# Moving the query and key rotation one chunk later in the recurrence of a hybrid decoder layer

## The chip, the cores and the metric

The kernel runs on one core of a Trainium2 chip, as one launch. The metric is the device time of that launch in microseconds (us). Before the change it was run three times: 2240.45, 2242.23 and 2244.01 us, median 2242.23 us. A further execution, recorded by the hardware profiler, took 2243.18 us by the same clock.

## The reference, cut to what matters

One layer, 1024 prompt tokens and 8 sample tokens together (1032 columns), model width 1024, float32. Each layer normalises its input with a condition-dependent scale and shift, multiplies by a wide input matrix, and runs two mixers on the result: attention with 8 heads, and a gated linear recurrence with 8 heads. Only the parts that the change touches:

```
qa = rope(rmsnorm(qa) * q_norm_g, pos); ka = rope(rmsnorm(ka) * k_norm_g, pos)   # per head, 2 halves of 64
oa = rmsnorm(attend(qa, ka, va)) * subln_g * 0.8                                  # per head, 128 wide
# recurrence over chunks of tokens, per head (S is the 128x128 state):
cum = cumsum(g); A = (q * decay) @ k;  o = A @ v + (q * exp(cum)) @ S
S   = exp(cum[-1]) * S + (k * exp(cum[-1] - cum)).T @ v
```

The rotation (rope) needs, for a piece of q or k: a multiplication by cos, a copy of the piece with its 32-row quarters exchanged, a multiplication of that copy by sin, a sum, and last a multiplication by the reciprocal root of the mean square, which comes from a product with a block matrix.

## The kernel before, in words

Every large product is done in three float32r products of split operands (high x high, high x low, low x high): one *piece* is 8 blocks of 3 products with 344 output columns, 24 products on TensorE (`product`, L172).

The first stage (`norm_stage`) normalises the input. TensorE adds up the squares (L350), makes the condition's scale and shift by `ada(k)` (L364, 32 small products) and `pick(k)` (L372), and in a loop over k = 0..7 issues `ada(k+3)`, `pick(k+2)` and `pieces(k)` (L385, 18 products, which need the k-th block of the normalised input, high and low: L337 on ScalarE, L474 on VectorE).

The second stage (`heads_stage`) goes over the 8 heads h. Each head has an attention part and then a recurrence part of 8 chunks k = 0..7 of 128 tokens. The dense pieces for later use are spread between them; in the recurrence chunk k carries one piece, `REC_PIECES[k]`. For heads 0 to 6 these are the queries, keys and values of the next head: piece u = 0..5 (three of q, three of k) is computed in the chunk before k = 0 (u = 0) and in chunk k = u - 1, the three of v in chunks 5, 6, 7. Head 7 has no next head (`no_next`).

Each engine has its own program in order, and waits on semaphores by hand; no planner is involved. In chunk k:

- **TensorE** waits for the operands of the chunk (`lv_k`, then L1192), makes the small products L1192 to L1202, transposes (L1207), before the change then adds up the squares of piece k - 1 (`qk_sums`, L1058 and L1059), computes its dense piece (L172), and closes with L1228 to L1232 (output and new state).
- **ScalarE** computes the decay levels of the next chunk (L916 to L922), copies the transpose (`kht`, L1015), finishes the levels (L927, L928), makes the high part of a square (L933), turns the sums into a reciprocal root (`qk_norm`, L818 and L820), then reads the dense piece out of PSUM (for q and k: square L813 and copy into `rg[u % 3]` L814), and copies the chunk's output (L1037).
- **VectorE** runs `assemble` (L1485 to L1492, after `kht`), `operands` of the next chunk (L1476, L1477), then before the change `squares_low` (L1508), `rope` (L1361, L1363) of piece k, `rope_end` (L1367) of piece k - 1, and `state` (L1500 or L1503).
- **GpSimd** computes level differences two chunks ahead (L1278, L1279) and multiplies the piece by cos (L1319). **SyncE's queue** issues the DMAs: the exchanged copy of a piece (`turn`, L706, four DMAs) once the piece is read and a `squares_low` is done, and the load of condition weights (L725).

Piece u is read into `rg[u % 3]`, one of three buffers. ScalarE may overwrite it when `rope_end` of piece u - 3 is done. That wait stands in the part of `piece` that reads q and k:

```
u = n - 12
act.wait_ge(qk_ready.sem, qk_ready.at(h, max(u - 2, 0)))
if u >= 2:
    act.wait_ge(sq_low.sem, sq_low.at(h, u - 1))
qk_piece(gq if kind == "q" else gk, bank, sq[u % 2][:, :], rg[u % 3][:, :])
```

`qk_ready` counts the `rope_end`s; these lines are not part of the diff. In the last chunk TensorE also adds up the squares of the attention's output (`attention_sums`, L1125 and L1126), inside the dense piece, and ScalarE makes the reciprocal root (L944, L946). Then the next head's `scores_of` (L1113) and `turn8` (L1119) follow.

Of the kernel before, what the change touches and what calls it, by code (L numbers as in the profile page):

```python
# [40 lines left out]
H = 8  # L41
# [155 lines left out]
def norm_stage(nc, a, c, x, hi, lo, mem, early, banks):  # L197
# [7 lines left out]
    with Stage(c) as ctx:  # L205
# [139 lines left out]
        @block.tensor  # L345
        def _(pe):
            def sums(p):
                pe.wait_ge(paired.sem, p + 1)
                for j in range(NP):
                    ins = pe.matmul(SP_[:, j, 0:TH], mean[:, :], sq[2 * p % 4][:, cols(j)], start=(p == 0), stop=(p == KT // 2 - 1))  # L350
                    if p == KT // 2 - 1:
                        ins.then_inc(summed.sem, 1)
                if p < KT // 2 - 1:
                    ins.then_inc(ms_used.sem, 1)

            def ada(k):

                if k >= 2:
                    pe.wait_ge(mod_in.sem, k - 1)
                for n in (2 * k, 2 * k + 1):  # L360
                    pe.wait_ge(ada_in[n % RING].sem, 16 * (n // RING + 1))
                    for r in range(KT):
                        quarter = slice(r % 4 * QUAD, (r % 4 + 1) * QUAD)
                        ins = pe.matmul(X[quarter, k % 2, n % 2 * P:(n % 2 + 1) * P], c["csil"][:, r, :],  # L364
                                        aw[n % RING][:, r * P:(r + 1) * P], start=(r < 4), stop=(r >= 4))
                ins.then_inc(ada_done.sem, 1)

            def pick(k):
                pe.wait_ge(ada_read.sem, k + 1)
                for n in range(2):  # L370
                    at = PICK_COL + n * QUAD
                    ins = pe.matmul(X[:, k % 2, at:at + CS], av[k % 2][:, n * P:(n + 1) * P], c["pick"][:, 0:CS], start=True, stop=True)  # L372
                ins.then_inc(picked.sem, 1)

            def pieces(k):

                pe.wait_ge(high.sem, k + 1)
                pe.wait_ge(low.sem, k + 1)
                w = slice(k * P, (k + 1) * P)
                for n, (t, j) in enumerate(EARLY_PIECES):  # L380
                    if k == 0 and j == 0:
                        pe.wait_ge(w_hi.sem, t + 1)
                        pe.wait_ge(w_lo.sem, t + 1)
                    for q, (wp, xp) in enumerate(((early["hi"], hi), (early["hi"], lo), (early["lo"], hi))):
                        pe.matmul(first[n], wp[t][:, w], xp[:, k, cols(j)], start=(k == 0 and q == 0), stop=(k == KT - 1 and q == 2))  # L385

            pe.wait_ge(mean_in.sem, 16)
            for p in range(KT // 2):
                sums(p)
            pe.wait_ge(csil.sem, 1)  # L390
            ada(0)
            ada(1)
            pe.wait_ge(pick_ready.sem, 1)
            pick(0)
            ada(2)
            pick(1)
            pe.wait_ge(lnd.sem, NP)
            for k in range(KT):
                if k + 3 < KT:
                    ada(k + 3)  # L400
                if k + 2 < KT:
                    pick(k + 2)
                pieces(k)

        @block.gpsimd
# [106 lines left out]
HIGH_AT = (4, 5)  # L512
SQUARES_AT = 6
SUMS_AT, SUMS_BEHIND = 7, 3
KEYS_AT = (3, 4, 5, 7)


# [21 lines left out]
def heads_stage(nc, a, o, c, d, xh, xl, early, banks, gate):  # L539
    with Stage(c) as ctx:  # L540
# [57 lines left out]

        def sum_bank(h, u):

            return u % 2 if u < 2 or h == H - 1 else 1

        def half(u):

            return slice((u % 2) * 512, (u % 2) * 512 + 512)

        def square_high(h, u):

            return osq_hi[1 if u >= 2 and h < H - 1 else 0][:, half(u)]
# [57 lines left out]
        def no_next(h):  # L667

            return h == H - 1
# [132 lines left out]
        def _(act):  # L802
# [137 lines left out]
            def o_norm(h, u):  # L940

                act.wait_ge(o_summed.sem, o_summed.at(h, u + 1))
                r = rstd_o[:, (u % 2) * 512:(u % 2) * 512 + 512]
                ch(act.activation(r, X[:, sum_bank(h, u), :], ACT.Ln, bias=c["eps"][:, 0:1]))  # L944
                ch.sync()
                act.activation(r, r, ACT.Exp, scale=-0.5).then_inc(o_rstd.sem, 1)  # L946

# [104 lines left out]
        def _(pe):  # L1052
# [54 lines left out]
            def scores_of(h, i):  # L1107
                nk = (i + 1) * P
                for m in range(2):
                    rows = slice(DH * m, DH * (m + 1))  # L1110
                    for b in range(0, nk, 512):
                        w = min(512, nk - b)
                        ins = pe.matmul(SP_[:, score_bank(i, m) + b // 512, 0:w], qT[rows, i * P:(i + 1) * P], kT[rows, b:b + w],  # L1113
                                        start=True, stop=True)
                ins.then_inc(scores.sem, 1)
# [6 lines left out]
            def o_sum(h, u):  # L1122
                pe.wait_ge(o_squared.sem, o_squared.at(h, u + 1))
                pe.wait_ge(o_high.sem, o_high.at(h, u + 1))
                pe.matmul(X[:, sum_bank(h, u), :], ones[:, :], square_high(h, u), start=True, stop=False)  # L1125
                pe.matmul(X[:, sum_bank(h, u), :], ones[:, :], osq_lo[:, half(u)], start=False, stop=True).then_inc(o_summed.sem, 1)  # L1126

            def attention_sums(h):
                if no_next(h):
                    pe.wait_ge(rows_ready.sem, 1)  # L1130
                else:
                    pe.wait_ge(qk_ready.sem, qk_ready.at(h, 6))
                o_sum(h, 0)
                o_sum(h, 1)

            for h in range(H):
                pe.wait_ge(qk_ready.sem, qk_ready.at(h, 0))
                scores_of(h, 0)
                pe.wait_ge(piece_read.sem, piece_read.at(h, 0))
                if h:  # L1140
                    pe.wait_ge(o_rstd.sem, o_rstd.at(h - 1, 2))
                turn8(Xf, vT).then_inc(v_turned.sem, 1)
                pe.wait_ge(o_read.sem, o_read.at(h, 0))
                pe.wait_ge(st_ready.sem, st_ready.at(h, 0))
# [38 lines left out]
                for k in range(NB):  # L1183
# [21 lines left out]
                    if REC_PIECES[k][0] in ADA_AT:  # L1205
                        ada(h, REC_PIECES[k][0])
                    pe.transpose(kht_ps, K[:, 0, :], ident[:, :]).then_inc(rec_done.sem, 1)  # L1207
                    if 0 < k <= 6 and not no_next(h):
                        pe.wait_ge(sq_high.sem, sq_high.at(h, k))
                        pe.wait_ge(sq_low.sem, sq_low.at(h, k))  # L1210
                        if k >= 3:
                            pe.wait_ge(qk_ready.sem, qk_ready.at(h, k - 2))
                        qk_sums((k - 1) % 2)
                    for n in REC_PIECES[k]:
                        piece(h, n, (SUMS_BEHIND, attention_sums, h) if k == SUMS_AT else None)
                    if k == 1 and no_next(h):
                        pe.wait_ge(sample_qkv.sem, sample_qkv.at(h, 1))
                        pe.wait_ge(sample_rec.sem, sample_rec.at(h, 1))
# [23 lines left out]
        def _(pool):  # L1242
# [53 lines left out]
            for h in range(H):  # L1296
# [16 lines left out]
                for k in range(NB):  # L1313
# [13 lines left out]
                    if k == SQUARES_AT:  # L1327
                        pool.wait_ge(pv_read.sem, pv_read.at(h, NB))
                        pool.wait_ge(o_normed.sem, o_normed.at(h, 0))
                        if not no_next(h):  # L1330
                            pool.wait_ge(qk_ready.sem, qk_ready.at(h, 5))
                        squares(h, oraw, 0)
                        squares(h, oraw, 1)
                    for n in REC_PIECES[k]:
# [13 lines left out]
        def _(dve):  # L1348
# [172 lines left out]
            for h in range(H):  # L1521
# [31 lines left out]
                for k in range(NB):  # L1553
                    assemble(h, k)
                    if k + 1 < NB:
                        operands(h, k + 1)
                    if k == 0:
                        use_sigmoid(h, len(SIGMOID) - 1)
                    if k == 7:
                        o_norm(h, 0)  # L1560
                        o_norm(h, 1)
                    if k < 6 and not no_next(h):
                        u, j = k, k % NP
                        if k:
                            squares_low(h, k)
                        dve.wait_ge(qk_cos.sem, qk_cos.at(h, u + 1))
                        dve.wait_ge(qk_turned[u].sem, qk_turned[u].at(h, 4))
                        rope(j, rg[u % 3][:, :], rt[u % 2][:, :])
                    if 0 < k <= 6 and not no_next(h):
                        u = k - 1  # L1570
                        dve.wait_ge(qk_rstd.sem, qk_rstd.at(h, u + 1))
                        if u == 0:
                            dve.wait_ge(sample_qkv.sem, sample_qkv.at(h, 1))
                            dve.wait_ge(kv_stored.sem, kv_stored.at(h, 2))
                        rope_end(u % NP, X[:, u % 2, 0:TH], rg[u % 3][:, :], qT if u < 3 else kT)
                    state(h, k)
                ch.reset()

# [2047 lines left out]
```

## Time and profile before

| | us |
|---|---|
| three runs, median (lowest, highest) | 2242.23 (2240.45, 2244.01) |
| the profiled execution, its own time | 2243.18 |
| its span, first to last instruction | 2241.4 |
| TensorE busy, products | 2210.7 (99%) |
| TensorE weight loads | 2100.9 (94%) |
| VectorE busy | 1557.2 (69%) |
| ScalarE busy | 1175.5 (52%) |
| GpSimd busy | 939.0 (42%) |
| the head read below, recurrence chunks 0 to 7 | 402.80 to 452.19 |

Busy time of TensorE is made of modelled ends, and small products overlap, so a short wait hides in it. For waits one reads the distance between the starts of instructions. The busy shares of the other engines are means over stages with different limits. The head read below is h = 2; times of rows are microseconds from the start of the span.

### The profile page before, as it was taken

To read this page: it belongs to the slowest core of one execution; us is meant where nothing else is said; L and a number is where in the kernel's file an instruction comes from. 1 tells how busy PE (TensorE), PEld (TensorE's weight loads), DVE (VectorE), ACT (ScalarE), POOL (GpSimd) and SP (SyncE) were. 2 spreads that over 40 slices of the span, in tenths; PEclk is the share of its full clock that TensorE was granted. 3 is DMA by queue.
4 is the path that set the end of the run, shared out by engine and by line. 5 is a ranking of instruction groups with operands and counts; after the bars stand their busy time and mean duration, and the time that the engine had idled before them with its cause. 6 is when DMAs were issued, how large, how long until landed. Compare 5 with 4: busy or idle time off the path is not lost. (4 is left out here: it accounts for less than half of the span.)

```text
span 2241.4 us, 47969 instructions
## 1 busy us (share of the span) xinstructions
PE 2210.7 (99%) x18881; PEld 2100.9 (94%) x18881; DVE 1557.2 (69%) x2574; ACT 1175.5 (52%) x2449; POOL 939.0 (42%) x1144
## 2 busy tenths in 40 slices
PE   7999999999999999999999999999999999999999
PEld 5899998989999989989988999999999999999999
DVE  5668687877778686876677515417988888876545
ACT  6567665766666666665444511114566666643110
POOL 1135262634444352626322224442165665635431
PEclk9999999999999999999999999999999999999999
DMA  8212122231213121222789623112344555485212
GB/s 310 86 55 94 46 86 67 59 105 56 99 50 105 44 88 56 70 89 88 273 301 367 244 44 121 48 48 93 123 179 185 188 186 185 175 317 190 86 48 95
DMA packets 103514, 288.35 MB, mean 129 GB/s; under 512 B 18426, under 2 KB 26490, under 8 KB 103290
## 3 DMA queue, kind: packets, MB, share of 16 engines
q1 hardware_dynamic: 102138, 281.09, 35.4%
q10 hardware_dynamic: 1152, 4.19, 0.5%
q8 instruction: 150, 2.46, 0.4%
q14 instruction: 74, 0.61, 0.1%
HBM read 213.18 MB, written 63.77 MB: 124 GB/s over the span
## 5 line engine op out<-in xcount | busy, mean ns | idle before, releaser
L172 PE MATMUL ps<-xn_hi,h_w_hi 128*128 128x344 f32 x1680 | 549.6, 327 | 2.2 <-PEq L205 0.9
L172 PE MATMUL ps<-xn_hi,h_w_lo 128*128 128x344 f32 x1680 | 536.5, 319 | 0.0
L172 PE MATMUL ps<-xn_lo,h_w_hi 128*128 128x344 f32 x1680 | 536.3, 319 | 0.0
L172 PEld LDWEIGHTS ps<-xn_hi,h_w_hi 128*128 128x128 f32 x1680 | 316.9, 189 | 35.2 <-issue 26.0
L172 PEld LDWEIGHTS ps<-xn_lo,h_w_hi 128*128 128x128 f32 x1680 | 315.6, 188 | 0.7
L172 PEld LDWEIGHTS ps<-xn_hi,h_w_lo 128*128 128x128 f32 x1680 | 315.7, 188 | 0.0
L1247 POOL TENSOR_TENSOR h_w_lo<-h_w_raw,h_w_hi 128x1024 fp32r<-128x1024 f32 x58 | 149.2, 2573 | 384.2 <-ACT h_w_hi L809 348.9
L3188 DVE SCALAR_TENSOR_TENSOR x<-ps,keep_mod,x 128x344 f32<-128x344 f32 x168 | 94.3, 570 | 163.3 <-PE ps L3025 100.7
L3025 PE MATMUL ps<-f_act_lo,f_d_hi 128*128 128x344 f32 x528 | 169.4, 321 | 0.0
L3025 PE MATMUL ps<-f_act_hi,f_d_lo 128*128 128x344 f32 x528 | 168.8, 320 | 0.0
L3025 PE MATMUL ps<-f_act_hi,f_d_hi 128*128 128x344 f32 x528 | 168.5, 319 | 0.1
L964 ACT ACTIVATE h_a_E<-ps,h_d_sm 128x256 f32<-128x256 f32 (+7 forms) x128 | 93.7, 739 | 112.9 <-DVE h_d_sm L1428 112.9
L1278 POOL TENSOR_TENSOR h_b_level_diff<-h_b_braw 128x64 f32<-128x64 f32 x320 | 96.2, 301 | 123.2 <-ACT ps L928 99.7
L2998 PE MATMUL ps<-f_t_hi,f_s_hi 128*128 128x258 f32 x456 | 128.8, 282 | 0.4 <-ACT ps L2729 0.4
L2998 PE MATMUL ps<-f_t_hi,f_s_lo 128*128 128x258 f32 x456 | 128.7, 282 | 0.0
L2998 PE MATMUL ps<-f_t_lo,f_s_hi 128*128 128x258 f32 x456 | 128.4, 282 | 0.0
L2646 ACT ACTIVATE h_w_hi<-h_w_raw 128x1024 fp32r<-128x1024 f32 x27 | 28.4, 1056 | 178.2 <-PE ps L172 168.9
L2633 POOL TENSOR_TENSOR f_s_lo<-f_s,f_s_hi 128x512 fp32r<-128x512 f32 x72 | 109.9, 1547 | 2.6
L3339 DVE TENSOR_TENSOR f_a_lo<-f_a,f_a_hi 128x512 fp32r<-128x512 f32 x57 | 77.2, 1356 | 37.8 <-POOL f_s L2617 21.4
L3025 PEld LDWEIGHTS ps<-f_act_hi,f_d_hi 128*128 128x128 f32 x528 | 99.2, 188 | 0.5 <-POOL f_d_lo L3129 0.4
L3025 PEld LDWEIGHTS ps<-f_act_lo,f_d_hi 128*128 128x128 f32 x528 | 99.3, 188 | 0.0
L3025 PEld LDWEIGHTS ps<-f_act_hi,f_d_lo 128*128 128x128 f32 x528 | 99.2, 188 | 0.0
(468 smaller groups left out, 6556.6 us busy)
## 6 DMA issues: line engine op xcount, KB each, us to landing
h_w_raw<-in_w_in SPq DMA_DIRECT2D x72, 512.0 KB, 3.6
y_rows<-f_y SPq DMA_DIRECT2D x44, 516.0 KB, 2.6
f_y_pair<-y_rows SPq DMA_DIRECT2D x22, 1032.0 KB, 5.4
h_d_ada_w<-in_w_ada SPq DMA_DIRECT2D x32, 512.0 KB, 4.4
g_vp<-in_cache_v SPq DMA_DIRECT2D x32, 512.0 KB, 6.2
f_a<-in_w_ffn SPq DMA_DIRECT2D x57, 256.0 KB, 2.6
g_kp<-in_cache_k SPq DMA_DIRECT2D x28, 512.0 KB, 7.7
h_w_raw<-in_w_mix SPq DMA_DIRECT2D x24, 512.0 KB, 3.5
```

The source lines that it names most:

```text
L172: ins = eng.matmul(out, w[:, k * P:(k + 1) * P], x[:, k, columns], start=(k == 0 and n == 0), stop=(k == n_k - 1 and n == 2))
L964: ins = act.activation(E[:, m, 0:nk], SP_[:, :, :].rearrange("p a b -> p (a b)")[:, 512 * score_bank(i, m):512 * score_bank(i, m) + nk], A ...
L1247: pool.tensor_tensor(wlo[w][:, :], raw[r][:, :], whi[w][:, :].bitcast(F32), ALU.subtract).then_inc(lo_done.sem, 1)
L1278: ch(pool.tensor_tensor(w[:, :, 0, :], v[:, :, 0, :], mid, ALU.subtract))
L2633: eng.tensor_tensor(wlow[n][i][:, :], wsum[n][i][:, :], whigh[n][i][:, :].bitcast(F32), ALU.subtract).then_inc(s_lo.sem, 1)
L2646: act.activation(whi[buf(n)][:, :], raw[n % 2][:, :], ACT.Copy).then_inc(w_hi.sem, 1)
L2998: ins = pe.matmul(bank, wp[:, w], xp[:, row, columns], start=(q in (1, 5) and k == 0 and r == 0), stop=(k == KH - 1 and r == 2), skip_grou ...
L3025: ins = pe.matmul(down_bank(n), wp[t % 3][:, at * P:(at + 1) * P], xp[place][:, k, cols(j)], start=(k == 0 and r == 0), stop=(k == n_k - 1 ...
L3188: ins = dve.scalar_tensor_tensor(out=xt[:, a0:a0 + n], in0=bank[:, 0:n], scalar=gain[:, 0:1], in1=xt[:, a0:a0 + n], op0=ALU.mult, op1=ALU.add)
L3339: dve.tensor_tensor(wlow[n][i][:, :], wsum[n][i][:, :], whigh[n][i][:, :].bitcast(F32), ALU.subtract).then_inc(a_lo.sem, 1)
```

## The change

Four things, all in the order and the waits of the engines' programs:

1. In the first stage TensorE gets 15 products of 128x128 with 128 columns whose result nobody reads (`keep_clock`), in groups of 2, 2, 1, 3, 1 and 6 between `ada`, `pick` and the first `pieces`.
2. In the recurrence VectorE rotates piece u in chunk u + 1 (before: chunk u), and `rope_end` of piece u comes in chunk u + 2 (before: chunk u + 1), right behind `operands`. `squares_low` moves behind `rope`.
3. The sums of squares of piece k - 1 move on TensorE from ahead of the dense piece of chunk k into it, behind its third block (9 products).
4. The sums of the attention's output go to two banks of the decay levels (`SP_` 2 and 3) rather than to the banks of the q and k sums. Their wait is now for the last `operands`; TensorE waits for their reciprocal roots ahead of the next head's scores rather than behind them. GpSimd's squares wait for the last `squares_low` rather than for the fifth `rope_end`.

```diff
@@ norm_stage, TensorE
+            def keep_clock(count):
+                for _ in range(count):
+                    pe.matmul(G[:, 0, 0:P], mean[:, :], mean[:, :], start=True, stop=True)
...
             ada(0)
+            keep_clock(2)
             ada(1)
             pe.wait_ge(pick_ready.sem, 1)
             pick(0)
+            keep_clock(2)
             ada(2)
+            keep_clock(1)
             pick(1)
+            keep_clock(3)
             pe.wait_ge(lnd.sem, NP)
             for k in range(KT):
                 if k + 3 < KT:
                     ada(k + 3)
+                if k == 0:
+                    keep_clock(1)
                 if k + 2 < KT:
                     pick(k + 2)
+                if k == 0:
+                    keep_clock(6)
                 pieces(k)
@@ heads_stage
+NQK = 2 * NP
...
         def sum_bank(h, u):
-            return u % 2 if u < 2 or h == H - 1 else 1
+            if u < 2:
+                return SP_[:, 2 + u, :]
+            return X[:, u % 2 if h == H - 1 else 1, :]
@@ TensorE
             def attention_sums(h):
                 if no_next(h):
                     pe.wait_ge(rows_ready.sem, 1)
-                else:
-                    pe.wait_ge(qk_ready.sem, qk_ready.at(h, 6))
+                pe.wait_ge(lv_k.sem, lv_k.at(h, NB))
                 o_sum(h, 0)
                 o_sum(h, 1)
             for h in range(H):
                 pe.wait_ge(qk_ready.sem, qk_ready.at(h, 0))
+                if h:
+                    pe.wait_ge(o_rstd.sem, o_rstd.at(h - 1, 2))
                 scores_of(h, 0)
                 pe.wait_ge(piece_read.sem, piece_read.at(h, 0))
-                if h:
-                    pe.wait_ge(o_rstd.sem, o_rstd.at(h - 1, 2))
                 turn8(Xf, vT).then_inc(v_turned.sem, 1)
...
+                    def piece_sums(u):
+                        pe.wait_ge(sq_high.sem, sq_high.at(h, u + 1))
+                        pe.wait_ge(sq_low.sem, sq_low.at(h, u + 1))
+                        if u >= 2:
+                            pe.wait_ge(qk_ready.sem, qk_ready.at(h, u - 1))
+                        qk_sums(u % 2)
+                    between = (SUMS_BEHIND, attention_sums, h) if k == SUMS_AT else None
                     if 0 < k <= 6 and not no_next(h):
-                        pe.wait_ge(sq_high.sem, sq_high.at(h, k))
-                        pe.wait_ge(sq_low.sem, sq_low.at(h, k))
-                        if k >= 3:
-                            pe.wait_ge(qk_ready.sem, qk_ready.at(h, k - 2))
-                        qk_sums((k - 1) % 2)
+                        between = (SUMS_BEHIND, piece_sums, k - 1)
                     for n in REC_PIECES[k]:
-                        piece(h, n, (SUMS_BEHIND, attention_sums, h) if k == SUMS_AT else None)
+                        piece(h, n, between)
@@ GpSimd
-                            pool.wait_ge(qk_ready.sem, qk_ready.at(h, 5))
+                            pool.wait_ge(sq_low.sem, sq_low.at(h, NQK))
@@ VectorE, in chunk k, behind assemble(h, k) and operands(h, k + 1)
-                    if k == 7:
-                        o_norm(h, 0)
-                        o_norm(h, 1)
-                    if k < 6 and not no_next(h):
-                        u, j = k, k % NP
-                        if k:
-                            squares_low(h, k)
-                        dve.wait_ge(qk_cos.sem, qk_cos.at(h, u + 1))
-                        dve.wait_ge(qk_turned[u].sem, qk_turned[u].at(h, 4))
-                        rope(j, rg[u % 3][:, :], rt[u % 2][:, :])
-                    if 0 < k <= 6 and not no_next(h):
-                        u = k - 1
+                    if 0 <= k - 2 < NQK and not no_next(h):
+                        u = k - 2
                         dve.wait_ge(qk_rstd.sem, qk_rstd.at(h, u + 1))
...
                         rope_end(u % NP, X[:, u % 2, 0:TH], rg[u % 3][:, :], qT if u < 3 else kT)
+                    if k == 7:
+                        o_norm(h, 0)
+                        o_norm(h, 1)
+                    if 0 <= k - 1 < NQK and not no_next(h):
+                        u = k - 1
+                        dve.wait_ge(qk_cos.sem, qk_cos.at(h, u + 1))
+                        dve.wait_ge(qk_turned[u].sem, qk_turned[u].at(h, 4))
+                        rope(u % NP, rg[u % 3][:, :], rt[u % 2][:, :])
+                    if 0 < k < NQK and not no_next(h):
+                        squares_low(h, k)
                     state(h, k)
```

## Rows read from the trace of the kernel before

**Rows 1.** The page, part 1: busy us, share of the span, instructions of each engine.
```profile
PE 2210.7 (99%) x18881; PEld 2100.9 (94%) x18881; DVE 1557.2 (69%) x2574; ACT 1175.5 (52%) x2449; POOL 939.0 (42%) x1144
```

**Rows 2.** The waits of PE over the whole span: total us, times, longest us.
```profile
PE ps L1192 <- DVEq L1479: 4.5, 8, 0.9
```

**Rows 3.** Windows, first stage: us, busy (instructions) PE PEld DVE ACT POOL, PEclk, DMA, GB/s.
```profile
24.50:27.97 3.47, 2.39 (x55) 1.89 (x54) 2.68 (x7) 1.72 (x6) 0.00 (x0) 1.00 1.03 412
27.97:34.80 6.83, 6.15 (x45) 5.27 (x34) 4.66 (x8) 5.61 (x8) 0.00 (x0) 0.50 1.03 394
```

**Rows 4.** Timeline of PE, first stage: start, us, what, count [idle before, releaser].
```profile
29.41 1.02 PE L372 MATMUL ps<-keep_pick,n_ada 128*128 128x9 f32 x4
31.09 0.62 PE L385 MATMUL ps<-xn_hi,h_w_hi 128*128 128x344 f32 x1 [0.65 <-issue]
...
35.77 1.08 PE L364 MATMUL ps<-n_ada_w,keep_csil 128*32 128x128 f32 x32
...
37.25 0.41 PE L385 MATMUL ps<-xn_hi,h_w_hi 128*128 128x344 f32 x1
...
40.27 1.08 PE L364 MATMUL ps<-n_ada_w,keep_csil 128*32 128x128 f32 x32
```

**Rows 5.** Timeline of ACT, first stage, in the round behind the first pieces.
```profile
36.92 0.39 ACT L300 ACTIVATE n_ada<-ps 128x256 f32<-128x256 f32 x1 [2.05 <-PE ps L364]
```

**Rows 6.** Timeline of PE: eight float32 products of 128 columns in a row.
```profile
396.20 1.04 PE L1119 MATMUL ps<-keep_ident,h_ib 128*128 128x128 f32 x8
```

**Rows 7.** Timeline of PE, head 2: starts of chunks 1, 2, 3, 4 and 7.
```profile
408.57 0.27 PE L1192 MATMUL ps<-h_fc,h_kk 128*32 128x32 f32 x8
...
415.08 0.27 PE L1192 MATMUL ps<-h_fc,h_kk 128*32 128x32 f32 x8 [0.51 <-DVEq L1479]
...
421.23 0.27 PE L1192 MATMUL ps<-h_fc,h_kk 128*32 128x32 f32 x8
...
427.15 0.27 PE L1192 MATMUL ps<-h_fc,h_kk 128*32 128x32 f32 x8
...
445.65 0.27 PE L1192 MATMUL ps<-h_fc,h_kk 128*32 128x32 f32 x8
```

**Rows 8.** Timeline of DVE, head 2, chunk 0 into chunk 1.
```profile
410.00 0.52 DVE L1361 TENSOR_TENSOR h_d_rt<-h_d_rt,h_sin 128x344 f32<-128x344 f32 x1 [0.81 <-POOL h_d_rg L1319]
...
413.89 1.08 DVE L1477 TENSOR_TENSOR h_b_LK<-ps,h_kk 128x896 f32<-128x896 f32 x1
```

**Rows 9.** Timeline of DVE, head 2, chunk 3 into chunk 4.
```profile
423.29 0.35 DVE L1485 TENSOR_TENSOR h_spot_near_products<-ps,h_d_near_mask 128x192 f32<-128x192 f32 x1
...
425.88 1.08 DVE L1477 TENSOR_TENSOR h_b_LK<-ps,h_kk 128x896 f32<-128x896 f32 x1
427.11 0.79 DVE L1508 TENSOR_TENSOR h_parts_sq_low<-h_parts_sq,h_parts_sq_high 128x344 fp32r<-128x344 f32 x1
...
428.91 0.51 DVE L1367 TENSOR_TENSOR h_qT<-h_parts_rg,ps 128x344 f32<-128x344 f32 x1
```

**Rows 10.** Timeline of ACT, head 2, chunks 1, 3, 4, and the end of chunk 7.
```profile
410.28 0.29 ACT L1015 ACTIVATE h_kht<-ps 128x128 f32<-128x128 f32 x1
...
423.90 0.54 ACT L818 ACTIVATE ps<-ps,keep_eps 128x344 f32<-128x344 f32 x1
...
426.49 0.27 ACT L860 ACTIVATE keep_mod<-ps,keep_vec 128x9 f32<-128x9 f32 x1 [1.58 <-PE ps L1094]
426.66 0.45 ACT L813 ACTIVATE h_d_sq<-ps 128x344 f32<-128x344 f32 x1
...
428.69 0.29 ACT L1015 ACTIVATE h_kht<-ps 128x128 f32<-128x128 f32 x1
...
450.54 0.63 ACT L946 ACTIVATE h_d_rstd_o<-h_d_rstd_o 128x512 f32<-128x512 f32 x1
```

**Rows 11.** Timeline of SP's queue (chunk 3) and of PE (behind chunk 7).
```profile
424.26 0.58 SPq L725 DMA_DIRECT2D h_d_ada_w<-in_w_ada  x1
...
452.19 0.49 PE L1113 MATMUL ps<-h_kT,h_qT 64*128 64x128 f32 x4
```

More of the change, by code:

```diff
@@ L943, in o_norm @@
                 r = rstd_o[:, (u % 2) * 512:(u % 2) * 512 + 512]
-                ch(act.activation(r, X[:, sum_bank(h, u), :], ACT.Ln, bias=c["eps"][:, 0:1]))
+                ch(act.activation(r, sum_bank(h, u), ACT.Ln, bias=c["eps"][:, 0:1]))
                 ch.sync()
@@ L1124, in o_sum @@
                 pe.wait_ge(o_high.sem, o_high.at(h, u + 1))
-                pe.matmul(X[:, sum_bank(h, u), :], ones[:, :], square_high(h, u), start=True, stop=False)
-                pe.matmul(X[:, sum_bank(h, u), :], ones[:, :], osq_lo[:, half(u)], start=False, stop=True).then_inc(o_summed.sem, 1)
+                pe.matmul(sum_bank(h, u), ones[:, :], square_high(h, u), start=True, stop=False)
+                pe.matmul(sum_bank(h, u), ones[:, :], osq_lo[:, half(u)], start=False, stop=True).then_inc(o_summed.sem, 1)
             def attention_sums(h):
```

## The prediction, made before the changed kernel was run

> **What bounds the kernel now.** I read the busy shares first: TensorE is busy 99% of the span and its weight loads 94%, the next engine 69% [rows 1]. So only what lengthens or shortens TensorE's own chain counts, and the waits of TensorE come second. Two places in that chain belong to the change. In the first stage the granted clock stands at 0.50 (1.2 GHz) from 27.97 to 34.80 us and at 1.00 (2.4 GHz) on both sides [rows 3]. In the recurrence TensorE waits for VectorE's operands at the start of a chunk: 4.5 us in 8 waits [rows 2]. In the head that I read it is 0.51 us at chunk 2 [rows 7]; by the distance of starts it is 0.59 (chunk 1 to 2 takes 6.51, chunk 3 to 4 only 5.92). Third I read VectorE and ScalarE chunk by chunk, because a busy share says nothing of who waits for whom within six microseconds.
>
> **Clock-keeping products.** Before the clock fell TensorE was busy 2.39 of 3.47 us, in short groups between waits [rows 3]. The 15 new products fill such waits. One costs about 0.11 us at full clock (eight in 1.04 us with 0.27 of tail: 0.77/7) [rows 6]. Fourteen stand ahead of waits on ScalarE, on a DMA or on the first pieces' input, and cost nothing at full clock; the one ahead of `pick(1)` delays what the first pieces wait for, by 0.11 to 0.2. What they can give back: the first `pieces` took 4.68 us (31.09 to 35.77), the next 3.02 (37.25 to 40.27) [rows 4]. The difference, 1.66, less 0.15, is 1.5 us. It is kept to the end of the stage, because in the later rounds ScalarE waits for TensorE and not the other way (2.05 us at 36.92) [rows 5]. If the clock falls all the same, seven of the products run at the half rate, 0.22 each by the `pick` products there (three steps in about 0.66 us) [rows 4]: they begin behind `pick(2)`, which ends near 30.6 with one product ahead of it, and six of them reach 31.9, so the pieces start 0.85 later. Bounds: -1.7 to +0.9; I take -1.5.
>
> A rule against this part: the Trainium skill (TensorE: Matmul & The Clock Gate, "Why this matters for your kernels") warns of throughput drops from one long idle gap of TensorE. The trace does not agree: no wait in this stretch is over 0.7 us and the clock fell [rows 4]. By the rule there would be nothing to keep and this part would give 0 rather than -1.5.
>
> **Rotation one chunk later: what it removes.** In chunk 0 VectorE waits 0.81 us for GpSimd's cos product before it can rotate [rows 8], and `assemble` of chunk 1 stands behind that. With nothing to rotate in chunk 0, `assemble` of chunk 1 starts as soon as ScalarE has copied the transpose, at 410.28 + 0.29 = 410.57 [rows 10]. From its start to the end of the operands it is 3.67 us (423.29 to 425.88 + 1.08) [rows 9], so they end at 414.27 rather than at 414.97 (413.89 + 1.08) [rows 8]. TensorE is ready 5.92 after 408.57, at 414.49: the wait of 0.59 in chunk 2 goes.
>
> **What it adds.** Piece u is read into one of three buffers, and ScalarE waits for `rope_end` of piece u - 3. In chunk k it reads piece k + 1, so it now needs `rope_end` of piece k - 2, and the new order puts that into the same chunk k, behind `assemble` and `operands`. Before, it was done a chunk earlier. Queued behind the waiting read on ScalarE are the output copy, the next levels and the copy of the next transpose, and VectorE's next `assemble` waits for that copy. This closes a ring in chunks 2, 3 and 4 (pieces 3, 4, 5):
>
> - ScalarE, from the start of the read to the end of the transpose copy: 426.66 to 428.69 + 0.29, 2.32 us [rows 10];
> - VectorE, `assemble` to the end of `operands`: 3.67; 0.15 until its next instruction starts (426.96 to 427.11); `rope_end` 0.51 [rows 9];
> - two handovers between engines. The one that rows show (operands to TensorE, 414.97 to 415.08) is 0.11 [rows 7, 8]; bounds 0 to 0.11 each, I take 0.035, since a copy of a whole tile is followed there by one more signal.
>
> The ring is 6.72 us. TensorE's own chunks are 6.15 (415.08 to 421.23) and 5.92 (421.23 to 427.15) [rows 7]. So the ring, not TensorE, sets the pace while it is closed:
>
> - chunk 2 starts at 414.49; `assemble` 1.9 later (2.06 in chunk 3 of the trace, less what VectorE no longer drags along), operands of chunk 3 end at 420.06, `rope_end` of piece 0 at 420.72. ScalarE could have read piece 3 at about 420.15 (5.43 after the start, as in chunk 3, and 0.23 for the condition products): it waits 0.57.
> - chunk 3 starts on time at 420.64. Transpose copied at 423.08, operands of chunk 4 at 426.79, chunk 4 at 426.90; TensorE was ready at 426.56: 0.34 lost.
> - one turn more: chunk 5 at 433.62, ready at 433.05: 0.57 lost.
> - one more: chunk 6 at 440.34, ready at 439.54: 0.80 lost.
> - from chunk 5 on ScalarE reads values, which don't wait for a rotation. Chunk 7 starts 6.15 later, at 446.49; before it was 445.65 [rows 7].
>
> That is +0.84 us for this head, gain of chunk 2 included. Seven heads have a next one: 7 x 0.84 = 5.9 us. With the handovers at both ends and `assemble` of chunk 2 0.2 earlier or later a head is +0.4 to +1.3, so 3 to 9 us.
>
> **The other edits, at nothing.** The sums inside the piece are the same two products. They come 1.4 us later (nine products of 0.16), and ScalarE's root starts at 423.90 now, waiting perhaps 0.1 for them; ScalarE has 1.58 us idle behind it, ahead of the piece [rows 10]. No row shows them inside a piece: bounds 0.05 either way for a sum, and where the ring sets the pace neither counts. The attention sums' new wait, for the last operands, is the one that opened their chunk. The wait ahead of the next scores is over at 451.17 (450.54 + 0.63) while these start at 452.19 [rows 10, 11]: 1.0 us of cover, behind which only the scores queue. In chunk 7 `rope_end` of piece 5 fits ahead of `o_norm`, whose roots end as late as that. GpSimd's squares wait for an event of the same chunk as before. SP's queue waits up to a `rope` longer (1.1 us) for `squares_low` before it issues a turn; the load behind it goes out at 424.26 [rows 11] for a use three chunks on, and the rotation itself now has a chunk to spare.
>
> **Sum.** -1.5 + 5.9 = +4.4 us. Against the profiled execution's own 2243.18 us (span 2241.4 and 1.8 outside) that is 2247.6; that execution lies 0.95 above the median of 2242.23, and the median gives 2246.6.
>
> **Rivals.**
>
> - *The ring does not close.* If `rope_end` is done before the piece is, the wait costs nothing, chunk 2's 0.59 goes and with it the later start waits, 0.3 in this head (chunk 4 to 7 take 18.50 us, where 5.92 and twice 6.15 are 18.22): -0.9 a head, 6.3 in all, with the clock -7.8: 2234.4, faster. For it: the 0.81 us that VectorE gains in chunk 0. Against it: 420.72 stands against 420.15. It decides when `assemble` of chunk 2 starts more than 0.57 earlier, which the transpose copy, 2.03 us behind the start of chunk 1, does not let it do. 21%.
> - *The clock falls all the same.* Ring as forecast, first stage +0.85: 5.9 + 0.85, 2249.0. For it: the waits stay waits, and the products fill only 1.65 us. Against it: six of them stand where the last 3.47 us were two thirds busy. 20%. The Trainium skill (the same page, "What's actually happening") has the observation window free-running, so that one kernel can differ from run to run; no single run here shows it.
> - *The ring closes but is paid from slack.* If the chain in front of chunk 2 is shorter by 0.4 and the handovers are at nothing, a head loses 0.2 and seven lose 1.4, against 1.5 gained: 2242.1. 15%.
>
> **How the numbers follow.** The forecast has 44%, its own range is 2243.5 to 2249.9 (3 to 9 less 1.5). Two tenths of a per cent, 4.5 us, is what a measurement of this kernel can tell from no change; so slower begins at 2246.7 and faster at 2237.7. Slower: half of the forecast and nearly all of the second rival, 0.41. Faster: the first rival, 0.21. Same: the rest, 0.38. The range takes in the forecast, the second and third rivals and the upper half of the first: 2234.5 to 2251.
>
> **What would show it.** In the changed profile: PEclk 1.00 from 20 to 40 us and first pieces in about 3.0 us (or 0.50 again); no wait at L1192 in chunk 2; ScalarE's L813 in chunks 2, 3, 4 starting right behind VectorE's L1367 rather than behind L860 or L865; starts of chunks 4 to 5 and 5 to 6 near 6.7 apart; chunk 1 to 7 near 37.9 rather than 37.08. If L813 follows the piece in those chunks, the ring is not there and the prediction is wrong.

## The result, and the profile after

The changed kernel takes 2248.70 us (median of 9 runs, 2248.05 to 2250.08), the kernel before 2242.91 beside it (9 runs): a ratio of 1.0025 [1.0014, 1.0035], 5.8 us slower, with an interval that lies above 1. The profiled execution took 2249.05 us, its span is 2247.2.

The page of the changed kernel, busy us, share and instructions [rows 1]:

```profile
PE 2215.7 (99%) x18911; PEld 2102.9 (94%) x18911; DVE 1612.3 (72%) x2574; ACT 1170.0 (52%) x2449; POOL 977.2 (43%) x1144
```

TensorE has 30 instructions more, two for each of the 15 products. VectorE has the same 2574 and is busy 55 us longer. That number misleads: only 17 of the 55 lie between the first head's recurrence and the last head's (681.2 us busy against 664.2). Nearly all of the rest lies behind that, where the two programs are alike in all but a few lines, and where the kernel before with the clock products alone (keep_only, below) is busy 34 us longer without being slower.

The first stage, windows of the changed kernel (columns as in [rows 3]), then TensorE's timeline (as in [rows 4]):

```profile
27.97:34.80 6.83, 6.78 (x73) 6.00 (x73) 4.84 (x10) 5.91 (x10) 0.00 (x0) 1.00 1.04 398
```

```profile
27.23 0.51 PE L372 MATMUL ps<-keep_pick,n_ada 128*128 128x9 f32 x4
27.59 0.91 PE L378 MATMUL ps<-n_mean 128*128 128x128 f32 x6
...
30.16 1.58 PE L378 MATMUL ps<-n_mean 128*128 128x128 f32 x12
31.79 0.39 PE L390 MATMUL ps<-xn_hi,h_w_hi 128*128 128x344 f32 x1
...
34.80 1.08 PE L364 MATMUL ps<-n_ada_w,keep_csil 128*32 128x128 f32 x32
```

The granted clock stays at 1.00 (2.4 GHz) where it was 0.50. The first pieces take 3.01 us (31.79 to 34.80) instead of 4.68, but start 0.70 later. Six products are twelve records (a record is one matrix instruction as the trace counts it) and 1.6 us.

The recurrence, head 2 of the changed kernel: TensorE's starts of chunks 1 to 7 (as in [rows 7]):

```profile
410.12 0.27 PE L1207 MATMUL ps<-h_fc,h_kk 128*32 128x32 f32 x8
416.06 0.27 PE L1207 MATMUL ps<-h_fc,h_kk 128*32 128x32 f32 x8
422.21 0.27 PE L1207 MATMUL ps<-h_fc,h_kk 128*32 128x32 f32 x8
428.58 0.27 PE L1207 MATMUL ps<-h_fc,h_kk 128*32 128x32 f32 x8
435.18 0.27 PE L1207 MATMUL ps<-h_fc,h_kk 128*32 128x32 f32 x8 [0.24 <-DVEq L1500]
441.79 0.27 PE L1207 MATMUL ps<-h_fc,h_kk 128*32 128x32 f32 x8 [0.35 <-DVEq L1500]
447.93 0.26 PE L1207 MATMUL ps<-h_fc,h_kk 128*32 128x32 f32 x7
```

Chunk 2's wait is gone (5.94). Chunks 3 to 6 start 6.37, 6.60 and 6.61 apart. Chunk 1 to 7 is 37.81; the mean of the seven heads is 37.83, against 37.09 before.

The waits of TensorE and of ScalarE, whole span (total us, times, longest) [rows 2]:

```profile
PE ps L1207 <- DVEq L1500: 6.2, 16, 0.5
```

```profile
ACT h_parts_sq L829 <- DVE h_qT L1388: 13.0, 14, 1.3
ACT h_d_sq L829 <- DVE h_qT L1388: 8.4, 7, 1.3
```

The second pair is new: 21 times (three in each of seven heads) ScalarE's read of a piece waits for VectorE's `rope_end`. One turn of that ring in head 2, ScalarE and then VectorE [rows 9, 10]:

```profile
429.16 0.46 ACT L829 ACTIVATE h_d_sq<-ps 128x344 f32<-128x344 f32 x1 [1.08 <-DVE h_qT L1388]
...
431.20 0.28 ACT L1031 ACTIVATE h_kht<-ps 128x128 f32<-128x128 f32 x1
...
435.76 0.46 ACT L829 ACTIVATE h_parts_sq<-ps 128x344 f32<-128x344 f32 x1 [1.17 <-DVE h_qT L1388]
```

```profile
431.52 0.36 DVE L1506 TENSOR_TENSOR h_spot_near_products<-ps,h_d_near_mask 128x192 f32<-128x192 f32 x1
...
433.99 1.08 DVE L1498 TENSOR_TENSOR h_b_LK<-ps,h_kk 128x896 f32<-128x896 f32 x1
435.22 0.51 DVE L1388 TENSOR_TENSOR h_qT<-h_parts_rg,ps 128x344 f32<-128x344 f32 x1
```

From the read to the end of the transpose copy 2.32; 0.04 over to VectorE; `assemble` to the end of `operands` 3.55; 0.15; `rope_end` 0.51; 0.03 back to the next read at 435.76. That is 6.60, the distance of the chunk starts.

And a place where nothing was expected, chunk 7 of head 2 in the changed kernel, VectorE beside GpSimd, then TensorE:

```profile
449.31 2.60 DVE L1384 TENSOR_TENSOR h_parts_rg<-h_parts_rg,h_d_rt 128x344 f32<-128x344 f32 x1
```

```profile
448.86 2.67 POOL L1268 TENSOR_TENSOR h_w_lo<-h_w_raw,h_w_hi 128x1024 fp32r<-128x1024 f32 x1
```

```profile
453.82 0.49 PE L1249 MATMUL ps<-h_AT,h_ibtok 128*128 128x128 f32 x2
```

The rope's addition of piece 5, 0.52 where nothing of GpSimd runs beside it, takes 2.60 and ends 0.38 behind the split; `assemble` of chunk 7 ends at 453.77, and TensorE starts the output product 0.2 late.

The balance at the first chunk of the last head (1030.84 against 1024.60, +6.2): first stage -0.80 (from this pair of executions, see keep_only); chunk 1 to 2 7 x -0.57; chunk 2 to 7 7 x +1.31; chunk 7 to the next head 7 x +0.27.

### The profile page after: what moved, and what is told of

Read it like the earlier page. It is cut to its first block and busy times, and to the rows that moved or that the text cites. A ratio compares the mean times of both kernels' runs of the same rounds, so it can differ in the third digit from the quotient of the medians.

```text
span 2247.2 us, 48037 instructions
## 1 busy us (share of the span) xinstructions
PE 2215.7 (99%) x18911; PEld 2102.9 (94%) x18911; DVE 1612.3 (72%) x2574; ACT 1170.0 (52%) x2449; POOL 977.2 (43%) x1144
## 5 line engine op out<-in xcount | busy, mean ns | idle before, releaser
L2654 POOL TENSOR_TENSOR f_s_lo<-f_s,f_s_hi 128x512 fp32r<-128x512 f32 x72 | 131.6, 1829 | 33.8 <-ACT f_s_hi L2742 31.2
L3150 POOL TENSOR_TENSOR f_d_lo<-f_d_raw,f_d_hi 128x1024 fp32r<-128x1024 f32 x22 | 58.1, 2640 | 92.7 <-ACT f_d_hi L2793 82.8
```

Of the source, the lines that this page charges most:

```text
L2654: eng.tensor_tensor(wlow[n][i][:, :], wsum[n][i][:, :], whigh[n][i][:, :].bitcast(F32), ALU.subtract).then_inc(s_lo.sem, 1)
L3150: pool.tensor_tensor(dlo[t % 3][:, :], draw[t % 3][:, :], dhi[t % 3][:, :].bitcast(F32), ALU.subtract).then_inc(d_lo.sem, 1)
```

## Experiments

Every ratio is to the kernel before, run on the same chip.

**Is the ring what costs the time? Open it.** Two kernels put `rope_end` elsewhere and leave the rotation where the change put it.

```diff
 # end_back: behind rope, as before       # end_first: ahead of assemble
-  rope_end(k-2)  (behind operands)       -  rope_end(k-2)  (behind operands)
   rope(k-1)                              +  rope_end(k-2)
+  rope_end(k-1)                             assemble(k)
```

> The changed kernel with one thing moved: rope_end of a piece stands right behind its rope again, in the chunk in which it stood before the change; the rotation itself stays one chunk later, and the sums, banks and clock products stay as changed. ScalarE's read of piece k+1 then waits for a rope_end of the chunk before. Theory (the ring costs the time): the ring is open, L829 of pieces 3, 4 and 5 follows the pieces and not L1388, no two chunk starts are 6.6 us apart, and with chunk 2's wait gone as well chunk 1 to chunk 7 takes 36.2 to 36.6 us rather than 37.8; seven heads give 8.4 to 11.2 us and what chunk 7 had lost at most 1.8 more: 2236 to 2240. Rival (the rotation's work on VectorE, stretched beside GpSimd's split and pushed onto the next chunk's start, costs the time): the same operations stand in the same chunks, so chunk 1 to 7 stays near 37.8 and the time at 2247 or above. Second rival (sums inside the piece or the attention sums cost it): also 2247 or above.

> The changed kernel with one thing moved: rope_end of piece k-2 stands ahead of assemble of chunk k instead of behind its operands. Theory (the ring): the wait of ScalarE's read is answered in the first two microseconds of a chunk, where the piece comes only 5.4 behind its start; the ring is open and chunk 1 to 7 takes 36.2 to 36.9 us; the upper end if rope_end, 0.51, now pushes assemble where VectorE did not idle ahead of it: 2236 to 2242. Rival (work beside GpSimd or the sums): 2247 or above, chunk 1 to 7 near 37.8.

Measured: end_back 2256.35 us, 1.0058 [1.0045, 1.0072]; end_first 2250.97, 1.0036 [1.0022, 1.0049]. Both slower than the changed kernel and on the side of the rivals; my theory missed by 16 and 9 us. The ring was open: in both, L829 waits for no `rope_end` in any chunk. Yet chunk 1 to 7 took 38.53 and 38.35. VectorE in end_back, head 1, from one chunk's operands to the next, and GpSimd beside it:

```profile
309.15 1.08 DVE L1498 TENSOR_TENSOR h_b_LK<-ps,h_kk 128x896 f32<-128x896 f32 x1
310.45 0.52 DVE L1382 TENSOR_TENSOR h_d_rt<-h_d_rt,h_sin 128x344 f32<-128x344 f32 x1 [0.21 <-DVE h_b_LK L1498]
311.00 1.12 DVE L1384 TENSOR_TENSOR h_d_rg<-h_d_rg,h_d_rt 128x344 f32<-128x344 f32 x1
312.16 0.51 DVE L1388 TENSOR_TENSOR h_kT<-h_d_rg,ps 128x344 f32<-128x344 f32 x1
...
315.74 1.08 DVE L1498 TENSOR_TENSOR h_b_LK<-ps,h_kk 128x896 f32<-128x896 f32 x1
```

```profile
310.45 1.30 POOL L1340 TENSOR_TENSOR h_d_rg<-h_d_rg,h_cos 128x344 f32<-128x344 f32 x1 [1.35 <-DMA h_d_rt<-h_d_rg]
```

VectorE waits for no other engine and needs 6.59 in this chunk, 0.6 of it because one rope operation stands beside the cos product and ends behind it. In end_first most of the loss comes from another place: chunk 6 to 7 takes 7.16 to 7.25 in every head (6.14 to 6.21 in the changed kernel), because GpSimd's squares meet an operation of `assemble` (L1510, 1.20 instead of 0.29 in head 2).

**The clock products alone.** The kernel before with `keep_clock` and its calls, nothing else.

> The kernel before with the 15 clock products alone. Theory (read from the trace of the changed kernel): the granted clock stays at full, the first pieces take 3.0 us instead of 4.7 but start 0.7 later, because a product takes two records of 0.11 each and delays the second pick; the heads' stage begins 0.8 us earlier and nothing takes that back: 0.7 to 1.0 us below the kernel before. Forecast on record: 1.5 below. Rival (the gain is used up behind the first stage, or the clock is a matter of the run): 0.3 below or less.

Measured: 2241.45 us, 0.9991 [0.9982, 1.0000]. The clock is 1.00 from 20 to 40 us, and the first head's recurrence begins at 153.28 rather than 154.40. The median is 2.0 below, where 0.7 to 1.0 was expected, and the interval is 0 to 4; this part hides none of the loss. How much it pays depends on the execution it is compared with: sums_only and sums_old_wait (next) have the first stage of the kernel before, and there the clock fell earlier (mean 0.66 and 0.78 from 24.50 to 27.97, where the kernel before has 1.00) and the first head's recurrence begins at 155.48 and 155.76. On the same two chips the kernels with the products begin it at 152.57 to 153.50. So the products give 0.8 to 2.9 by the pair of executions, and not one fixed amount.

**The other edits alone.** The kernel before with the piece's sums inside the piece, the attention sums in the scores' banks, and GpSimd's wait as changed (sums_only); then the same with that one wait as it was (sums_old_wait).

```diff
-  pool.wait_ge(sq_low.sem, sq_low.at(h, NQK))        # sums_only
+  pool.wait_ge(qk_ready.sem, qk_ready.at(h, 5))      # sums_old_wait
   squares(h, oraw, 0)
```

> The kernel before with the other edits alone: the piece's sums inside the dense piece, the attention sums in the scores' banks with their waits, GpSimd's squares behind the last squares_low; rotation and first stage as before. Forecast on record: nothing, within 0.05 us for a sum in 42 chunks, so at most 2 us either way. Theory: within 1 us of the kernel before. Rival (these edits bring the loss, the ring only looks like it): 4 us or more above it.

> The kernel before with the sums inside the piece and the attention sums in the scores' banks, but with GpSimd's squares waiting for rope_end of piece 4 as before, not for the last squares_low. With the latter the squares began 1.6 us earlier in chunk 6, beside the rope, which took 1.24 instead of 0.52, and chunk 7 started 0.85 us late in each of seven heads. Theory (that wait alone brought the 6 us): chunk 6 to 7 is back at 6.15 and the time within 1 us of the kernel before. Rival (the sums or banks cost it): 2247 or above.

Measured: sums_only 2249.95 us, 1.0031 [1.0022, 1.0041]; sums_old_wait 2243.61, 1.0001 [0.9992, 1.0010]. So sums_only landed on the rival's side, and sums_old_wait says which edit did it. The sums and banks cost nothing, as forecast. GpSimd's wait costs chunk 6 nothing in the changed kernel (6.16 to chunk 7 in the mean; what it does to chunk 7 there no run shows); in the old order the last `squares_low` stands ahead of `rope`, so the squares run beside it, and in end_first they meet `assemble`. VectorE and TensorE in sums_only, head 3, chunk 6 and the start of 7:

```profile
568.72 1.24 DVE L1371 TENSOR_TENSOR h_parts_rg<-h_parts_rg,h_d_rt 128x344 f32<-128x344 f32 x1
```

```profile
574.69 0.27 PE L1194 MATMUL ps<-h_fc,h_kk 128*32 128x32 f32 x8 [0.97 <-DVEq L1487]
```

The same loss as the whole change, from another place: had I stopped at this run, I would have blamed the sums.

**Ring or contention?** GpSimd's cos product left out, with the ring and without it.

```diff
-  pool.tensor_tensor(rg[k % 3], rg[k % 3], cos[...], ALU.mult).then_inc(qk_cos.sem, 1)
+  pool.sem_inc(qk_cos.sem, 1)
```

> The changed kernel without GpSimd's product of a piece with cos in the recurrence (its event is still given), so the rotation leaves that factor out; all else as changed. What is asked: is the pace of chunks 4 and 5, 6.60 us in every head, set by the ring, or by VectorE's operations that are stretched beside GpSimd's cos product (a rope operation of 0.52 takes up to 1.1 there)? Theory (the ring): the stretch goes, VectorE idles that much longer for ScalarE's copy of the transpose, and chunks 4 to 5 and 5 to 6 still take 6.60; chunk 1 to 7 37.7 to 37.8, 2247 to 2249 us. Rival (VectorE's stretched work): both fall to 6.0 to 6.2, chunk 1 to 7 to 36.3 to 36.7, the time to 2238 to 2242.

> The same cos product left out of the kernel in which rope_end stands right behind its rope again, so without the ring. That kernel's chunks took 6.5 to 6.6 us and VectorE had no idle in them: with every operation unstretched its loop was 6.01, with one rope operation beside the cos product (1.12 to 1.25 instead of 0.52) 6.6. Theory (under the ring lies VectorE's full loop, and beside GpSimd it is as long as the ring): without the cos product VectorE's loop is 6.01 and TensorE's 5.93 and 6.15 set the pace; chunk 1 to 7 36.3 to 36.9 us; with what chunk 7 still loses 2241 to 2246. Rival (the order itself is too long, whatever runs beside it): chunk 1 to 7 stays at 38.1 or above, 2254 or above.

Measured: after_no_cos 2246.24 us, 1.0012 [1.0003, 1.0021]; end_back_no_cos 2238.42, 0.9975 [0.9966, 0.9984]. Both times lie below what was expected, by 0.8 and 2.6 us, but the chunks settle the question. With the ring, chunks 4 to 5 and 5 to 6 still take 6.60 to 6.62, and chunk 1 to 7 37.59. The 0.24 a head that the cos product did cost lies in the turn before, chunk 3 to 4: 6.36 in the mean with it, 6.12 without. Without ring and cos product chunk 1 to 7 is 36.23 to 36.24 in all seven heads, TensorE's own 5.94 and 6.15 in turn. VectorE in that kernel, head 2:

```profile
423.77 1.08 DVE L1498 TENSOR_TENSOR h_b_LK<-ps,h_kk 128x896 f32<-128x896 f32 x1
425.07 0.52 DVE L1382 TENSOR_TENSOR h_d_rt<-h_d_rt,h_sin 128x344 f32<-128x344 f32 x1 [0.21 <-DVE h_b_LK L1498]
425.62 0.52 DVE L1384 TENSOR_TENSOR h_parts_rg<-h_parts_rg,h_d_rt 128x344 f32<-128x344 f32 x1
...
429.81 1.08 DVE L1498 TENSOR_TENSOR h_b_LK<-ps,h_kk 128x896 f32<-128x896 f32 x1
```

Its loop is 6.04 with no wait for another engine in it, as long as TensorE's mean of 5.94 and 6.15. In this order VectorE has no slack in a full chunk, so an operation that is held up there moves TensorE.

**Remove chunk 2's wait without rotating later.** The kernel before with the clock products; in chunk 0 GpSimd's cos product stands ahead of the next differences (cos_first).

> The kernel before with the clock products and one swap on GpSimd: in chunk 0 the cos product of piece 0, whose input has landed at 405.2, stands ahead of the differences of chunk 2 instead of behind them (405.9 to 408.6). No rotation is moved. Theory: VectorE's wait of 0.81 in chunk 0 goes, and chunk 2's start with it (0.58 in each of seven heads); the differences end 0.5 later at 409.1, just ahead of ScalarE's use at 409.2; no ring is closed: chunk 1 to 7 36.4 to 36.6 us, 2236.5 to 2238 with the 0.8 of the first stage. Rival (the chunks behind are VectorE's anyway and take the gain back, or the later differences hold ScalarE): chunk 1 to 7 stays at 37, 2240.5 to 2241.5.

Measured: 2252.59 us, 1.0043 [1.0030, 1.0057]; missed by 15 us, and 11 above the rival. ScalarE in head 2:

```profile
412.04 0.71 ACT L929 ACTIVATE ps<-h_b_level_diff 128x640 f32<-128x640 f32 x1 [0.83 <-POOLq L1294]
```

The cos product had to wait for its DMA (it began at 407.86, 3.15 behind the chunk's start), the differences behind it ended at 412, and ScalarE, with the transpose copy behind it in its queue, waited for them. Chunk 1 to 2 grew from 6.51 to 7.35 in the mean: to 6.62 to 6.64 in three heads, this one among them, and to 7.56 to 8.18 in the four where the cos product began only 3.83 to 4.48 behind the chunk's start. GpSimd's differences were as urgent as what I put ahead of them.

**Wait only where the value is read.** The kernel before with the clock products; `rope` waits for the cos product ahead of its second operation (two_waits).

```diff
-  dve.wait_ge(qk_cos.sem, ...); dve.wait_ge(qk_turned[u].sem, ...)
-  rt = rt * sin;  rg = rg + rt
+  dve.wait_ge(qk_turned[u].sem, ...);  rt = rt * sin
+  dve.wait_ge(qk_cos.sem, ...);        rg = rg + rt
```

> The kernel before with the clock products and one thing more: VectorE's rope waits for the turned piece ahead of its first operation, as it must, and for GpSimd's cos product only ahead of the second, which alone reads it. Nothing is moved on GpSimd. In chunk 0 the first operation can start at 409.2 in place of 410.0 (head 2), the second at 410.0. Theory: the wait of 0.81 shrinks by one operation, 0.55, less what the first is stretched beside the cos product (up to 0.6); chunk 2's start wait of 0.58 falls to 0.05 to 0.4 in seven heads: chunk 1 to 7 36.5 to 36.9 us, 2237.5 to 2240.5 us. Rival (the stretch beside GpSimd takes it all, or later chunks take it back): chunk 1 to 7 at 37.0, 2241 to 2242.5.

Measured: 2240.05 us (11 runs), 0.9987 [0.9978, 0.9996]: below both kernels, at the upper end of what was expected. Chunk 1 to 2 is 6.22 instead of 6.51, but the chunks behind take half of that back: chunk 1 to 7 is 36.92, against 37.05 in keep_only. The last head begins 0.8 us sooner than in keep_only; by the times alone this kernel can't be told from keep_only (0.9991 [0.9982, 1.0000]). VectorE and GpSimd, head 2, chunk 0:

```profile
408.41 1.23 DVE L1375 TENSOR_TENSOR h_d_rt<-h_d_rt,h_sin 128x344 f32<-128x344 f32 x1
409.68 0.52 DVE L1378 TENSOR_TENSOR h_d_rg<-h_d_rg,h_d_rt 128x344 f32<-128x344 f32 x1
```

```profile
408.14 1.12 POOL L1332 TENSOR_TENSOR h_d_rg<-h_d_rg,h_cos 128x344 f32<-128x344 f32 x1 [0.24 <-POOL h_b_level_diff L1292]
```

The first operation starts early and is held past the end of the cos product at 409.26: half of the wait comes back as a stretch.

**Chunk 7.** The changed kernel; GpSimd's last split of a head waits until chunk 7 is assembled (late_split).

> The changed kernel with one wait more: GpSimd's last split of a head (the next head's first weights, 2.67 us in chunk 7) waits until VectorE has assembled chunk 7. What is asked: where do 0.26 us a head behind chunk 7 come from? Theory (contention): the rope operation that took 2.60 beside that split takes 0.52 to 1.1, assemble of chunk 7 ends before TensorE needs it, and from chunk 7 to the next head's chunk 0 it is 81.45 rather than 81.70: 1.5 to 1.8 us below the changed kernel, 2246.5 to 2247.5. Rival (the rotation of piece 5 in chunk 7 is too much by itself, or the next head now waits for its weights): 81.70 or above, 2248.5 or above.

Measured: 2250.04 us, 1.0031 [1.0019, 1.0043], no gain that the times show. The place was right and the cure was not: in head 2 the addition takes 0.52 again and TensorE no longer waits at L1249, but the split now stands beside VectorE's `o_norm`, 0.75 before:

```profile
451.77 2.45 DVE L1537 SCALAR_TENSOR_TENSOR h_d_oraw<-h_d_oraw,h_subg,h_d_rstd_o 128x512 f32<-128x512 f32 x1 [0.15 <-ACT h_d_rstd_o L962]
```

Chunk 7 to the next head is 81.62, against 81.73 in the changed kernel and 81.45 before. The 0.17 that are left arise 12.5 us behind the start of chunk 7, in the next head's attention. GpSimd's next squares now begin behind `o_norm`, 7.5 to 7.7 behind that start instead of 7.0, and VectorE's last weighing operation, 0.35 in every head before, meets them in every head:

```profile
458.56 1.45 DVE L1462 SCALAR_TENSOR_TENSOR h_a_E<-h_a_E,h_d_sm 128x128 f32<-128x128 f32 x1
```

TensorE's transposition of the weights waits for it. The changed kernel has the same 1.43 to 1.45 there.

**The whole change without ring and contention.** `rope_end` right behind `rope`, and the cos product a chunk later too, beside `operands` (cos_late).

```diff
-  if k < 6: turn_cos(k)              # piece k, as soon as it is turned
+  if 0 < k < 6: turn_cos(k - 1)      # behind the differences
+  if k == 6: turn_cos(5)             # ahead of the squares
```

> The kernel with rope_end right behind its rope (no ring), and the cos product of a piece one chunk later on GpSimd too, behind the differences, where VectorE multiplies operands that come from PSUM; for piece 5 ahead of the squares of chunk 6. Nothing is left out. Theory (ring and contention are all there is): no rope operation stands beside a cos product for more than 0.4 us; VectorE's loop is 6.0 to 6.3, chunk 1 to 7 36.3 to 36.9 us, and with chunk 7 as before this edit (0.3 a head) 2238 to 2243 us. Rival (the stretch only moves to the operands or to assemble): chunk 1 to 7 37.5 or above, 2248 or above.

Measured: 2241.93 us (11 runs), 0.9995 [0.9986, 1.0004]: 14 us below end_back, level with the kernel before (which lacks the clock products). VectorE and GpSimd in head 2:

```profile
418.33 1.08 DVE L1502 TENSOR_TENSOR h_b_LK<-ps,h_kk 128x896 f32<-128x896 f32 x1
419.62 0.52 DVE L1386 TENSOR_TENSOR h_d_rt<-h_d_rt,h_sin 128x344 f32<-128x344 f32 x1 [0.21 <-POOL h_d_rg L1340]
```

```profile
418.51 0.93 POOL L1340 TENSOR_TENSOR h_d_rg<-h_d_rg,h_cos 128x344 f32<-128x344 f32 x1 [0.24 <-POOL h_b_level_diff L1300]
```

Beside an operand product, one of whose inputs is in PSUM, the cos product stretches nothing. Chunk 1 to 7 is 36.7 to 36.9 in five heads, but 37.5 in heads 3 and 6, where the squares of chunk 6, now 0.9 later, meet an operation of `assemble`. VectorE and GpSimd in head 3:

```profile
565.01 1.19 DVE L1514 TENSOR_TENSOR h_AT<-h_spot_near_sum,h_spot_same_mask 128x128 f32<-128x128 f32 x1
565.01 1.04 POOL L1306 TENSOR_TENSOR h_d_rstd_o<-h_d_oraw 128x512 f32<-128x512 f32 x1
```

It is a tie: in all seven heads the two start within 0.01 us of each other. In heads 3 and 6 VectorE's takes 1.19 instead of 0.29 and GpSimd's 1.04; in the other five VectorE's takes 0.29 and GpSimd's 1.18 or 1.19. Chunk 7 loses 0.8 in the same two heads (82.23 and 82.24 to the next) and nothing in the others (81.41 to 81.43).

## Why the prediction came out as it did

- *The ring.* Right in place, wait and pace: a wait of L829 on L1388 in three chunks of each head, 6.60 us a turn where 6.72 was forecast (`assemble` to `operands` 3.55, not 3.67), chunk 1 to 7 +0.74 a head, not +0.84. after_no_cos shows that it, and not the stretched operations, sets the pace of chunks 4 and 5; without the cos product +0.50 of the +0.74 stays.
- *Chunk 2's wait.* Gone in all seven heads, 0.57 where 0.59 was forecast.
- *The clock products.* The clock held. The term came to -0.8 against this execution of the kernel before, not -1.5, but the two other first stages without the products give -2.0 to -2.9 (see keep_only), so its size is not refuted; its working is. I priced a product at 0.11 from the eight of [rows 6], which are transposes and take one record each; a float32 product takes two, 0.22 to 0.26 (twelve records, 1.58 us). So six of them, with a pick that came 0.8 later, held the first pieces back by 0.70 where I allowed 0.15. The rule of the Trainium skill that I weighed (TensorE: Matmul & The Clock Gate, "Why this matters for your kernels") would have left nothing to keep; keep_only disagrees, the clock stayed up there.
- *"In chunk 7 `rope_end` of piece 5 fits ahead of `o_norm`."* This step failed: +0.27 a head, 1.9 us in all. What I had not costed is that with the rotation a chunk later `rope` of piece 5 runs in TensorE's chunk 7 as well, beside GpSimd's split.
- *The sum.* +5.8 measured (+6.2 up to the last head's first chunk), +4.4 forecast. Between these two executions the ring cost 0.7 less than forecast over seven heads and the clock gave 0.7 less; that these two cancel is luck. What is left is chunk 7's 1.9, which stood in the sum as nothing.
- *The first rival, 2234.4 if the ring does not close.* Its mechanism can be had, its number was wrong. It assumed that with the ring open nothing is late next. With it open VectorE's loop was (6.59 beside the cos product in the chunk shown), and the time 2251 to 2256. Only without the cos product did it come near: 2238.4. What the prediction lacked is a sum of VectorE's whole chunk, and the question of who runs beside each operation that is moved.

The rows of before held the sign of it: a VectorE operation of the rope takes 0.52 [rows 8], and `squares_low`, on tensors of the same size, 0.79 [rows 9]. I read the 0.79 as a duration and not as an operation that had been held; in the same trace `squares_low` takes 0.52 where GpSimd is idle.

What stays open: what the clock products are worth in one execution, since the clock fell at another time in each of the three profiles without them; and what decides the tie in cos_late.

## What to carry to other kernels

Before moving work on an engine that has no slack, add up its whole loop, and for each moved operation name what runs beside it on the engine that can hold it up: where a moved operation lands matters as much as what waits for it. When a wait closes a ring, ask what the next longest loop is before counting the ring's excess as a gain. And move a wait to the instruction that reads the value before moving the work itself: here that gave about 0.8 us by the trace, too little for the times to confirm, where moving the work lost 5.8.

## What the runs showed of the hardware

- VectorE and GpSimd hold each other up. An operation of VectorE on two SBUF tensors, 0.52 alone, took 1.12 to 1.24 beside a GpSimd operation of 1.12 to 1.30 (end_back, two_waits, sums_only) and 2.60 beside one of 2.67, and in each case ended 0.37 or 0.38 behind it; where both began together, GpSimd's took 1.30 instead of 0.92 (end_back). Operations with one input in PSUM (`rope_end` 0.51, operands 1.08) and the reduction (0.50 to 0.53) were the same beside GpSimd as alone. The Trainium skill says just this (SBUF — State Buffer, "Who interferes with whom"): a VectorE instruction with two SBUF inputs contends with a GpSimd one that reads SBUF, and the second to issue is blocked until the first is done. The traces agree with it, the reduction included; weighed before the change, it would have told that the rope must not meet the cos product or the split.
- The contention shows as a longer duration of the instruction, not as a wait, and the busy time of a page does not tell whether it matters: VectorE was busy 1612.3 us in the changed kernel, 1557.2 in the kernel before, but 1591.9 in keep_only and 1599.8 in two_waits, which are no slower than the kernel before.
- A single SBUF input does not make every VectorE operation safe: in the kernel before a scaling of 128x2 elements (L1428, one SBUF tensor and no second one) took 0.17 alone and up to 1.24 beside GpSimd.
